# RWKV-7 group begin on one core: the filling behind the scores of either half taken out, and x of half 0 issued between the turns of the two halves

## What is computed

```
def step(s, inp):
    r_t, w_t, k_t, v_t, a_t, b_t = inp
    sa = einsum('bhvk,bhk->bhv', s, a_t)
    s = s * w_t[:, :, None, :] + sa[..., None] * b_t[:, :, None, :] + v_t[..., None] * k_t[:, :, None, :]
    o = einsum('bhvk,bhk->bhv', s, r_t)
    return s, o
```

## Time and profile before

| | before |
|---|---|
| median of 3 runs | 2285.06 us (2283.15 to 2286.97) |
| the profiled execution, its own time | 2286.44 us |
| its span in the profile | 2284.7 us |
| mean granted TensorE clock | 0.996 of full speed |
| TensorE busy | 2229.0 us (98%), weight loads 2105.0 us (92%) |
| VectorE, ScalarE, GpSimd busy | 964.3, 431.9, 554.2 us |
| bytes moved by DMA | 171.16 MB, 75 GB/s on average |

### The profile page before, as it was taken

The page is one execution under the profiler, slowest core; times in us unless marked ns, Lnnn a source line. Parts: engine busy times, 40 slices in busy tenths (PEclk is TensorE's granted clock), DMA queues, the critical chain, the costliest instruction groups (busy, mean ns, idle before and its releaser), DMA issues.

```text
span 2284.7 us, 47115 instructions
## 1 busy us (share of the span) xinstructions
PE 2229.0 (98%) x20858; PEld 2105.0 (92%) x20858; DVE 964.3 (42%) x1199; ACT 431.9 (19%) x795; POOL 554.2 (24%) x288
## 2 busy tenths in 40 slices
PE   8999999999999999999999999999999999999998
PEld 6899888888888799889999988999999999999997
DVE  5333654636545354354443154544114314412523
ACT  4111414214142211163111032110000000000011
POOL 0233201101011022123333301333333333323331
PEclk9999999999999999999999999999999999999999
DMA  7211201112011093236113134111111111111112
GB/s 282 84 45 37 64 20 55 41 39 69 20 58 38 26 272 139 92 137 254 39 44 120 37 133 154 37 46 46 46 37 46 46 46 39 44 46 46 46 37 88
DMA packets 57712, 171.16 MB, mean 75 GB/s; under 512 B 8416, under 2 KB 24160, under 8 KB 54752
## 3 DMA queue, kind: packets, MB, share of 16 engines
q1 hardware_dynamic: 46816, 143.63, 19.0%
q10 hardware_dynamic: 10752, 25.35, 3.2%
HBM read 140.90 MB, written 28.05 MB: 74 GB/s over the span
## 4 chain that ended last, share of the span: by engine, by line
PE 87%; DVE 5%; DMA 3%; ACT 2%; issue 1%; SPq 1%; POOL 0%; ACTq 0%; DVEq 0%; POOLq 0%
PE ps L388 87%; DMA w_raw<-w 2%; DVE F L1162 1%; SPq L2235 1%; DVE TT L1162 1%; ACT F L1765 1%; DMA vc<-vc 1%; DVE F L1165 0%; DVE F L1168 0%; DVE Sst L1165 0%; ACT L1765 0%; DVE Xst L1162 0%; DMA par<-par 0%; POOL w_split L379 0%; PE ps L1032 0%
## 5 line engine op out<-in xcount | busy, mean ns | idle before, releaser
L388 PE MATMUL ps<-A_s,w_split 128*128 128x364 f32 (+1 forms) x6192 | 1082.5, 333 | 8.6 <-ACT zstg L1765 6.8
L388 PEld LDWEIGHTS ps<-A_s,w_split 128*128 128x128 f32 x6192 | 1030.1, 189 | 36.0 <-issue 14.3
L388 PE MATMUL ps<-B_s,w_split 128*128 128x364 f32 (+3 forms) x4032 | 672.4, 328 | 0.5 <-POOL w_split L379 0.5
L388 PEld LDWEIGHTS ps<-B_s,w_split 128*128 128x128 f32 x4032 | 667.7, 188 | 3.6 <-issue 1.3
L376 POOL CAST w_split<-w_raw 128x1024 fp32r<-128x1024 f32 x142 | 153.1, 1078 | 1684.9 <-PE ps L388 1596.5
L379 POOL TENSOR_TENSOR w_split<-w_raw,w_split 128x1024 fp32r<-128x1024 f32 x142 | 400.9, 2823 | 11.4
L1162 DVE TENSOR_TENSOR F<-ps,F 128x1092 f32<-128x1092 f32 (+3 forms) x52 | 62.8, 1208 | 420.6 <-PE ps L388 420.6
L1765 ACT ACTIVATE B_s<-T 128x1092 fp32r<-128x1092 f32 x32 | 35.9, 1121 | 621.6 <-DVE T L1168 621.6
L1168 DVE SCALAR_TENSOR_TENSOR T<-ps,rsx 128x1092 f32<-128x1092 f32 x32 | 41.5, 1296 | 205.2 <-PE ps L388 197.1
L1162 DVE TENSOR_TENSOR B_s<-T,B_s 128x1092 fp32r<-128x1092 f32 x32 | 105.9, 3309 | 1.1
L1162 DVE TENSOR_TENSOR T<-T 128x1092 f32<-128x1092 f32 x58 | 104.5, 1803 | 2.1 <-ACT T L1765 0.9
(11 more groups left out here) (208 smaller groups left out, 1794.1 us busy)
## 6 DMA issues: line engine op xcount, KB each, us to landing
w_raw<-w SPq DMA_DIRECT2D x144, 512.0 KB, 3.6
z<-zstg SPq DMA_DIRECT2D x83, 182.0 KB, 1.9
F<-z SPq DMA_DIRECT2D x16, 546.0 KB, 6.9
w_raw<-w SPq DMA_DIRECT2D x7, 1024.0 KB, 10.3
kc<-kc SPq DMA_DIRECT2D x7, 1024.0 KB, 4.8
vc<-vc SPq DMA_DIRECT2D x7, 1024.0 KB, 4.8
F<-x SPq DMA_DIRECT2D x8, 546.0 KB, 9.7
Zs<-z SPq DMA_DIRECT2D x16, 273.0 KB, 20.2
```

The costliest lines, as they stand in the source:

```text
L388: return pe.matmul(out, lhsT, rhs, start=start, stop=stop, skip_group_check=skip)
```

## The change

Both fills of two steps behind the scores of the halves are taken out of `group`. The turns of half 0 are followed at once by x of level 1 of half 0, then come the turns of half 1 and x of level 1 of half 1; the loop over the levels begins with av and yz for level 1. The mark "turned" of a group is dropped; no program reads it.

```
                         for part in range(3):
                             scores(p, h, u, part)
-                    fill(2)
                 for u in range(2):
                     turns(p, 2 * g + u, u)
-                mark(p, g, "turned")
+                    x_level(p, 2 * g + u, u, NB, 1)
                 for lv in range(1, LEVELS):
-                    for u in range(2):
-                        x_level(p, 2 * g + u, u, NB, lv)
+                    if lv > 1:
+                        for u in range(2):
+                            x_level(p, 2 * g + u, u, NB, lv)
                     if lv == 1:
                         for u in range(2):
                             av(p, 2 * g + u, u, NB)
```

## The result

The change makes the kernel slower, by 0.4%: 2294.55 us, the median of six runs (2292.70 to 2298.28), against 2286.43 for the kernel before in six runs beside it (2283.15 to 2286.97). The ratio is 1.004 with a 95% interval of 1.0028 to 1.0052, so some 8 us are lost where 2.4 were forecast, and the time lies above the forecast range (2283.8 to 2292.5). The profiled execution of the changed kernel took 2292.7 us for a span of 2290.9. That is the fastest of the six, and its span is 6.2 us longer than that of the profiled execution before.

The account below looks back on a forecast made before the run. TensorE, busy for 98% of the span, was taken as the bound. Saving 13.8 us in the begins and paying 16.2 in the tail gave +2.4 net: 2287.5 us on the median, range 2283.8 to 2292.5.

Parts of the forecast that it names:

- The fill budget and the tail: Side projection: no fill step is removed, 32 move to the last fill run, which grows by 16.2 us.
- (a) to (f): Steps of a first group's begin, first score to yz: 7.93 us after, 9.55 before, 1.6 saved.
- (d): First group: VectorE's masks of half 1 become the bound; its turns wait from 4.53 to 4.94 us.
- (e) and (f): First group's end: ScalarE's TK copies done at 7.32 us, its av read by about 7.8, yz at 7.93.
- The second group: Its begin, last state matmul to yz, falls from 8.82 to 7.16 us; first scores wait for ScalarE's t1 reads.
- The sum of the begins: Eight begins fall from 74.87 to 60.4 us; with a 0.69 us stall expected to recur, 13.8 saved.
- rival 2: Instruction supply bounds the begins between scores of half 0 and yz: a stall each, +5.5 us, 2293.0; chance 0.15.
- The rotary stage: Shifted weight-tile boundaries there: at most 1.0 us won or one more wait of 1.9; zero taken.
- Work that moves with it, costed at nothing: Units, copies and stores keep their places; shifted weight-tile boundaries matter only in the DMA-bound rotary stage; zero taken.
- rival 4: Clock halved in the begins without their large matmuls: 1.3 us each, +10 us, 2297.9; chance 0.02.
- rival 1: Waits in the begins forecast too long; saving nears its bound of 21 us: -4.6, 2280.5 us; chance 0.05.
- rival 3: Rotary stage falls badly: a further 1.9 us wait and a late retention weight, +3 us, 2290.4; chance 0.06.

Follow-up runs that it names:

- experiment 3: Changed kernel with VectorE's centring of the next head issued ahead of the two low parts in the norms; 2287.73 us, ratio 1.0005 to the kernel before.
- experiment 6: Changed kernel with 24 more fill steps, one weight tile, ahead of the pairs; 2290.70 us, ratio 1.0019 to the kernel before.
- experiment 9: Changed kernel with centring ahead of the low parts and eight more fill steps behind retention's sample turns; 2287.10 us, ratio 1.0004 to the kernel before.
- 8: Changed kernel timed again, nothing altered; 2293.62 us, ratio 1.0034 to the kernel before.
- 4: Changed kernel with eight more fill steps behind retention's sample turns, moving the tile boundary back; 2286.16 us, ratio 0.9996 to the kernel before.
- 5: Kernel before, groups untouched, with sixteen more fill steps behind retention's sample turns; 2291.15 us, ratio 1.0017 to the kernel before.
- 1: Kernel before with only the two fills taken out, x of level 1 in its old order; 2292.85 us, ratio 1.0024 to the kernel before.
- 10: Kernel before with the fills out, x in its old order, eight more fill steps behind retention's sample turns; 2286.25 us, ratio 1.0003.

## Why the prediction was wrong

Point by point, by its own steps:

- **The fill budget and the tail**: right. 237 fill matmuls in 39.71 us in the last run, where about 237 and 16 us more were forecast; 15.9 it was.
- **(a) to (f), a first group**: right where no stop falls in it: yz at 7.79 for 7.93. The wait of (d) came where it was put and was shorter (0.18 for 0.41), and ScalarE paced the end as (e) and (f) said.
- **The second group**: right, 7.02 for 7.16, its scores waiting 0.39 us for ScalarE's reads of t1.
- **The sum of the begins**: 11.1 us saved in place of 13.8. The begins without a long stop show that the steps were right. The eight take 3.4 us more than the 60.4 of the forecast, and the waits with no releaser in them are 3.45 together; 0.7 of that the forecast had set aside, which leaves the missing 2.7. This is rival 2 in part: three begins have such a stop of 0.8 us or more, the other five none so long. Its time, 2293.0, is by chance near the profiled run's 2292.7, but the mechanism didn't decide: experiment 3 keeps the stops and loses nothing, 6 moves them and keeps the wait in the norms and the loss.
- **The rotary stage**: the forecast took zero between -1.0 and +1.9. TensorE gained 5.0 us there. Its wait of 1.86 for a split, one of 2.03 for a finished unit's copy (which itself stood behind a store, `z<-zstg`) and a halved stretch of the clock were gone. The forecast's bound, "at most 1.0 us is won", took the end of VectorE's last rotary product as fixed. It isn't: that product ended 80.7 us behind the stage's start before and 76.5 after (851.04, and retention starts at 851.14), since VectorE, though it began 1.3 us later, waited 3.5 us less for loads of z and lost 2.0 less beside GpSimd's splits. Retention then gave back 2.8, of which 2.00 is one new wait for the split of the tile that used to be waited for in the rotary stage:

```profile
856.12 0.77 PE L388 MATMUL ps<-A_s,w_split 128*128 128x364 f32 x3 [2.00 <-POOL w_split L379]
```

  Net 2.2 us better than zero, so this term was off as well and by luck hid part of the error.
- **The step that failed** is "Work that moves with it, costed at nothing", in its sentence that the shifted boundaries matter in one stage, the rotary one. They were followed as demand for weight data alone: when is a tile wanted, and is its DMA in time. But a boundary also starts GpSimd's split, two instructions of 3.4 to 5.5 us together, and that slows VectorE. The place where VectorE was on the path with low parts queued ahead of a centring, the norms, was never looked at. It cost 5.6 us in the profiled run. By the medians it is 3.9 to 8.4: 6.5 from experiment 9 to 8, 6.8 and 8.4 from 3 and 4 to the changed kernel (timed apart from them), 4.3 and 3.9 from the kernel before to 5 and 6 (in 6 with the rest of the change, which 9 shows to be worth nothing measurable).
- **The halved clock** was priced as a rival in the begins (rival 4), where it did not come; each of the eight was at 1.00. In the profiles of experiments 1, 9 and 10 it did come, once each, in the first begin of pair 3, which took 10.8 to 10.9 us there for 8.94 in the changed kernel. With the new wait in the norms it came for 6.8 us in the profile of the changed kernel and of 1, for 3.4 in those of 8 (the same kernel again) and 5, and not at all in that of 6. This may be part of why the loss spreads; with so few profiled executions it isn't shown.
- **Two prices of rivals** are a little off by their own terms: 16.2 - 21 is -4.8 and not -4.6 (rival 1), and 2287.5 + 3 is 2290.5 (rival 3). Nothing hangs on them.

The sum of the profiled run closes: -18.5 up to retention (11.1 in the begins, 5.0 in the rotary stage, and the rest in other places, one halved stretch of the clock fewer behind the chains among them, not followed further), +2.8 retention, +15.9 fills, +5.6 norms, +0.5 behind. That is 6.2. The median stands at +8.1 (six runs) and +7.0 (ten runs); which of the variable terms, clock or stops, makes up that last microsecond or two was not settled.

## What to carry to other kernels

Work that is cut into tiles has a phase, and taking steps out in one place shifts it in every stage behind: list all that a tile boundary starts (the load, the split on another engine, the copy of the unit), and look in each later stage at what it will fall beside. In an engine's queue, put what the bounding engine waits for ahead of what nobody waits for yet; that one exchange made the collision harmless here, with the boundary left where it did the harm. And where work is only moved to another place of the same engine, the net is a small difference of two terms (here 11.1 us saved in the begins, 15.9 paid in the last fill run), so that side effects can decide the sign.

## What the runs showed of the hardware

**VectorE and GpSimd take turns.** The two low parts that took 5.52 us are 2.128 and 3.465 us long by the trace's view of their tile:

```profile
L1162 DVE TENSOR_TENSOR B_s<-xm,B_s x2: 2128/2796/3465, 973.4 to 975.5; 128x1092 fp32r<-128x1092 f32 x2
```

Alone one takes about 1.25 (2.49 for two). The first began at 973.41 and ended about 1.15 behind the end of GpSimd's cast at 974.39; the second ended at 978.93, 1.16 behind the end of GpSimd's product at 977.77. That product took 3.30 us where in experiment 3 it took 2.38; when it began, at 974.47, the first low part had 1.07 us to go. So an instruction of one engine runs for most of its time behind that of the other, not beside it. The Trainium skill, "SBUF — State Buffer", section "SBUF: two separate sides", says just this: a VectorE instruction with two SBUF inputs and a GpSimd instruction that reads SBUF take an exclusive lock on a shared pair of ports, and the loser stands for the whole instruction. The trace agrees, to about 0.15 us. It also agrees for the instruction that is exempt by that rule: the centring, which reads PSUM and one SBUF tensor, took 1.28 at 981.62 in the kernel before, in the middle of the product of a split (980.63 to 983.92). Retention shows another case, qd<-F,qdc of 0.63 us stretched to 2.83 beside a split of 2.34:

```profile
L1162 DVE TENSOR_TENSOR qd<-F,qdc x2: 628/1727/2826, 851.6 to 853.8; 128x512 f32<-128x512 f32 x2
```

**Stops without a releaser keep their places.** Over the pairs the packets of the instruction queue, 16 KB each, come in the changed kernel once in about 255 TensorE records, weight loads counted (79 packets from 284 to 786 us), and never closer than 3.3 us. The wait that ended at 693.53 ended 2.2 us behind the start of such a packet at 691.35. The other waits of 0.4 us or more without a releaser in that trace ended 2.3 to 2.9 us behind one. Kernels with the same sequence of instructions stop at the same instruction, for different lengths (x of half 0 in pair 3: 1.39, 1.35, 2.07, 1.81 and 2.06 us in the changed kernel and experiments 3, 4, 8 and 9), and experiment 6, whose stream is shifted, doesn't stop there. That these are waits for instructions is inferred from this, not shown by a view. The Trainium skill, "Runtime: NRT & Kernel Launch", section "Instruction fetch mechanics", calls a crossing of such a block mostly hidden. Most crossings here were; if these stops are such crossings, one cost up to 2.07 us in the begins without a fill.

**A stall of the same length doesn't always halve the clock.** TensorE waited 3.57 or 3.58 us at the same place of its program in five profiled executions. The granted clock was 0.50 for 6.8 us, from about 2 us into the wait (changed, 1), or for 3.4 us, from 0.7 to 0.8 us behind its end (5, 8), or it stayed at 1.00 (6). The changed kernel and 8 are one kernel, so the difference lies in the execution.
